# Another order within a tick on VectorE and ScalarE, in the stage that weaves attention into the projections

## The reference

```python
def project(x, norm_mix, w_in, q_norm, k_norm):
    p = rmsnorm(x, norm_mix) @ w_in
    q, k, v, z, xbc, dt_raw = jnp.split(p, [...], axis=-1)
    q = rmsnorm(q.reshape(b, t, N_HEADS_A, HEAD_DIM), q_norm)
    k = rmsnorm(k.reshape(b, t, N_HEADS_A, HEAD_DIM), k_norm)

def dilated_branch_prompt(q, k, v, rel_bias, window, dil):
    logits = jnp.einsum('gnqhd,gnkhd->gnhqk', qb, kb) * ATTN_SCALE
    logits = jnp.where(valid[None, :, None], logits + bias[None, None], -jnp.inf)
    m = jnp.max(logits, axis=-1, keepdims=True)
    pr = jnp.exp(logits - m)
    den = jnp.sum(pr, axis=-1)
    o = jnp.einsum('gnhqk,gnkhd->gnqhd', pr, vb) / jnp.swapaxes(den, 2, 3)[..., None]

def causal_conv(xbc, prior, conv_w, conv_b):
    out = sum(xpad[:, i:i + t] * conv_w[i] for i in range(CONV_WIDTH)) + conv_b
    return jax.nn.silu(out), xpad[:, t:]
```

## Time and profile before

| | us |
|---|---|
| median of 3 runs | 1942.02 |
| lowest and highest | 1933.88, 1943.04 |
| profiled execution | 1942.02 |
| its span | 1940.1 |
| TensorE busy | 1851.5 (95%) |
| VectorE busy | 1405.9 (72%) |
| ScalarE busy | 887.6 (46%) |
| POOL busy | 1099.8 (57%) |

### The profile page before, as it was taken

How to read it: one execution, slowest core, us unless ns; L and a number is a source line. 1 busy time by engine, 2 the same in 40 slices (tenths; PEclk the granted TensorE clock), 3 DMA queues, 4 the chain that set the end, 5 groups by cost and what they waited for, 6 DMA issues and landing times.

```text
span 1940.1 us, 33409 instructions
## 1 busy us (share of the span) xinstructions
PE 1851.5 (95%) x12776; PEld 1700.9 (88%) x12776; DVE 1405.9 (72%) x1897; ACT 887.6 (46%) x1610; POOL 1099.8 (57%) x846
## 2 busy tenths in 40 slices
PE   8999999998888999989997999999999999999999
PEld 7999999887777888855556789989999999999999
DVE  5788830787677766569987655798767779877876
ACT  5433412576566777456663002343333344444442
POOL 4588740777676777424444223335555557777774
PEclk9999999999999999979998999999999999999999
DMA  4444433543443443389995535114343357444442
GB/s 172 148 169 179 172 136 94 126 130 95 109 110 95 134 125 111 113 287 327 328 319 177 185 145 189 73 61 183 123 162 144 137 212 285 149 152 156 143 134 92
DMA packets 139097, 309.31 MB, mean 159 GB/s; under 512 B 31659, under 2 KB 65323, under 8 KB 135228
## 3 DMA queue, kind: packets, MB, share of 16 engines
q1 hardware_dynamic: 114924, 270.60, 41.5%
q10 hardware_dynamic: 24016, 36.58, 5.5%
HBM read 222.42 MB, written 93.28 MB: 163 GB/s over the span
## 4 chain that ended last, share of the span: by engine, by line
PE 58%; DVE 11%; POOL 5%; issue 5%; ACT 3%; DMA 0%; ACTq 0%; DVEq 0%; POOLq 0%
PE ff_ps L2594 31%; PE dense_ps L973 7%; PE wo_psa L2429 5%; POOL att_p L920 3%; PE att_t_ps L1002 2%; PE wo_psb L2561 2%; PE wo_psa L2561 1%; PE att_s_ps L991 1%; PE att_s_ps L992 1%; DVE sa_vlo L1961 1%; POOL w_lo L235 1%; PE ssd_in L1638 1%; DVE silu_half L1118 1%; PE sa_s L1551 1%; DVE ssd_m L1879 1%
## 5 line engine op out<-in xcount | busy, mean ns | idle before, releaser
L2594 PE MATMUL ff_ps<-ff_set,ff_wring 128*128 128x264 f32 x5376 | 661.5, 286 | 8.4 <-DVE ff_set L3206 3.5
L2594 PEld LDWEIGHTS ff_ps<-ff_set,ff_wring 128*128 128x128 f32 x5376 | 658.9, 189 | 10.5 <-DVE ff_set L3206 3.9
L920 POOL TENSOR_SCALAR att_p<-att_p,att_rden 128x128 f32<-128x128 f32 (+7 forms) x128 | 242.3, 1901 | 118.2 <-DVE att_rden L1060 118.1
L2263 POOL TENSOR_TENSOR ff_wring<-const,ff_wring 128x256 fp32r<-128x256 f32 (+1 forms) x192 | 212.6, 1111 | 146.5 <-ACT ff_wring L2759 145.9
L2759 ACT ACTIVATE ff_wring<-const 128x256 fp32r<-128x256 f32 (+1 forms) x192 | 93.5, 489 | 222.0 <-PE ff_ps L2594 108.4
L3228 DVE TENSOR_TENSOR h<-h,ff_ps 128x528 f32<-128x528 f32 x192 | 133.2, 700 | 49.9 <-PE ff_ps L2594 47.1
L1180 ACT ACTIVATE att_pThi<-att_t_ps 128x512 fp32r<-128x512 f32 x192 | 93.5, 487 | 133.6 <-PE att_t_ps L1002 125.3
L1078 DVE CUSTOM_DVE_ANT_0 att_p<-att_s_ps,att_bias 128x128 f32<-128x128 f32 (+7 forms) x128 | 95.3, 754 | 57.8 <-PE att_s_ps L992 51.9
L1065 DVE TENSOR_TENSOR att_pTlo<-att_t_ps,att_pThi 128x512 fp32r<-128x512 f32 x192 | 104.5, 552 | 41.2 <-ACT att_pThi L1180 41.0
L973 PE MATMUL dense_ps<-u_hi,w_hi 128*128 128x352 f32 x480 | 115.0, 341 | 10.3 <-DVE conv_pre L1092 3.1
L2263 POOL TENSOR_TENSOR ff_wring<-wo_raw,ff_wring 128x256 fp32r<-128x256 f32 (+1 forms) x72 | 83.5, 1159 | 61.8 <-ACT ff_wring L2759 61.8
(11 more groups left out here) (366 smaller groups left out, 4316.2 us busy)
## 6 DMA issues: line engine op xcount, KB each, us to landing
tmp_r_sets<-h SPq DMA_DIRECT2D x16, 1848.0 KB, 5.9
ff_setraw<-tmp_r_sets SPq DMA_DIRECT2D x56, 528.0 KB, 5.5
sa_k<-in_cache_k SPq DMA_DIRECT2D x32, 640.0 KB, 8.9
sa_v<-in_cache_v SPq DMA_DIRECT2D x40, 512.0 KB, 4.7
w_raw<-in_w_feat SPq DMA_DIRECT2D x36, 512.0 KB, 6.4
out_qk<-proj_out SPq DMA_DIRECT2D x16, 528.0 KB, 8.0
tmp_bias_rows<-tmp_table ACTq DMA_DIRECT2D x8, 1024.0 KB
att_bias<-tmp_bias_rows SPq DMA_DIRECT2D x16, 512.0 KB, 3.4
```

Source lines behind the costliest of these rows:

```text
L920: pool.tensor_scalar(slot(h, qt), slot(h, qt), rden[:, qt, :], None, ALU.mult).then_inc(normed, 1)
L2263: pool.tensor_tensor(w_set(n)[:, 1], operand(q, m), w_set(n)[:, 0].bitcast(F32), ALU.subtract).then_inc(fw_split, 1)
L2594: mm = pe.matmul(ff_ps[:, (b + g) * 512:(b + g) * 512 + HG], ws[:, wi, k, :], xs[:, xi, k, g * HG:(g + 1) * HG], start=(opens and k == 0 a ...
```

## The change

On VectorE, `keep_low` now comes ahead of `bias_min` in a tick, and `invert` comes ahead of `evict`, `add_out` and `split_v`. On ScalarE, `split_out` comes ahead of `keep_high`. No instruction is added or removed, and the loops of TensorE, POOL and SyncE are as they were.

```diff
@@ VectorE @@
             for n in range(FIRST - 1, END + 1):
                 if n == FIRST + 1:
                     split_v(0)
+                if n in piece:
+                    keep_low(n, *piece[n])
                 for h, qt in score.get(n, ()):
                     bias_min(h, qt)
-                if n in piece:
-                    keep_low(n, *piece[n])
+                if n - 1 in score:
+                    invert(score[n - 1])
                 for d in evict_at.get(n, ()):
                     evict(d)
                 if n in ends:
@@
                 if n >= 0 and h < NH and n % TICKS == 9:
                     split_v(h)
-                if n - 1 in score:
-                    invert(score[n - 1])
                 for d, t in tap_at.get(n, ()):
                     convolve(d, t)
@@ ScalarE @@
+                if n in ends:
+                    split_out(*ends[n])
                 if n in piece:
                     keep_high(n, *piece[n])
-                if n in ends:
-                    split_out(*ends[n])
                 for h, qt in score.get(n - 1, ()):
                     exponent(h, qt)
```

## The result

The changed kernel takes 1962.38 us (median of 6 runs, 1957.66 to 1966.71) against 1940.88 us (6 runs, 1933.88 to 1943.04): ratio 1.0119, 95% interval 1.0103 to 1.0137. By the medians it is slower by 21.5 us, by the ratio by 23 us (20 to 27); 1944.7 us was forecast. The profiled execution took 1962.54 us with a span of 1960.6, so it stands for the median as that of before did.

The account below looks back on a forecast made before the run. TensorE, busy 454.4 of 490 us in the stretch from 340 to 830 us, was taken as the bound. Terms -2.0 + 3.0 - 1.1 + 2.2 - 0.6 + 1.2 = +2.7 on 1942.02 gave 1944.7 us, range 1931 to 1956.

Parts of the forecast that it names:

- R2: Slower: reductions pushed back in VectorE's classes 7 and 9 set each head's pace; 18.6 us, 1960.6 us; chance 0.17.
- part 2, on add_out: On VectorE, the output sum behind the reciprocal: +0.69 us counted at waits for tile 4's reduction, 0 in later heads.
- (b): On VectorE, tile 4's reduction behind `keep_low` of its own tick: +0.6 us for each of five TensorE waits, +3.0.
- Its reading that the rows don't agree on the normalising: POOL's normalising at 589.48 ran beside the tap of 589.31, which still took 1.32 us, so no port exclusion there.
- Part 1 (a): TensorE's transpositions wait less for `keep_low` of two ticks earlier: three of 8 stalls keep their gain, -2.0 us.
- Part 1 (c): `keep_low` fills VectorE's holes before scores, so evictions come earlier at two of three waits for silu_half: -1.1 us.
- Part 2, evictions: Evictions behind `invert` on VectorE: +1.6 us at tick 42, 0.3 each at ticks 109 and 121, sum +2.2.
- Part 3: `split_out` ahead of `keep_high` on ScalarE: split waits' gain 0, eviction at tick 98 later by 1.2 us.
- The argument against R2: VectorE waits 50 times for scores in the stretch, more than three times a head, so is late only in places.
- R2's own test: It decides if TensorE meets the reduction of tile 4 late in more than 8 heads, as 8 x 1.24 = 9.9.
- TensorE's busy time and the granted clock stay.: Expected sign in the profile: no change in TensorE's busy time or granted clock; no us were put on it.
- The prediction's own sign of being wrong: TensorE's waits in the stretch changing by more than 10 us, or its waits for att_min falling.

Follow-up runs that it names:

- the last three edits: Kernel before with class 6's taps ahead of add_out and invert, with no taps in class 8, and with both: 0.9994, 0.9995 and 1.0003.

## Why the prediction was wrong

The forecast was +2.7 us with +24 as the outermost bound; measured is 21 to 23. The case that came true is rival R2 (1960.6 us), which had 0.17. Its mechanism is right in the main, and that its number is so near is in part luck: it priced 18.6 us of waiting, and 14.7 us of waiting came, with 6.7 us of a slower TensorE that no case had.

**The step that failed first: part 2, on add_out: "In the later heads VectorE has room: 0."** It counted 0.69 us inside five waits of (b) and nothing elsewhere. The run with this move alone is 0.69% slower; it lost 13.7 us, 5.6 of them as idle time of TensorE, with 12 hidden waits behind `keep_low` of class 7 in place of 6. The reciprocal waits for an exponent, and everything behind it waits too; the sum filled that hole for nothing, and behind it delays what follows. I looked at whether VectorE has idle time in these heads, which it has, and not at where: it lies ahead of the reciprocal and ahead of the scores of tile 4, and the moved sum falls between them, ahead of tile 7's reduction, whose result ScalarE waits for, and `keep_low`, for which TensorE's next transposition waits. In the head shown the length was off too: 1.21 and 1.26 us instead of 0.68, as the sum now starts beside POOL's w_lo subtraction. In the run with this move alone that subtraction runs from 718.34 for 1.29 us; the sum starts at 718.92 and ends 0.55 after it. In the full change it is 721.81 for 1.30, and 0.54. The Trainium skill (SBUF — State Buffer, "SBUF: two separate sides") says that such a pair exclude each other at their shared port, and here the trace agrees but for 0.14 us, as the 0.54 and 0.55 us left after the subtraction are less than the sum's 0.68. The prediction applied this to the taps, and not to the sum, which it had moved onto that subtraction. Its reading that the rows don't agree on the normalising was wrong: there the normalising paid (the last section has the rows).

**Part 1 (b), 5 x 0.6 = +3.0.** It priced `keep_low` ahead of tile 4's reduction at its own 0.55 us because its input stood ready at 593.95. That was read from a head with a tap there; in a light head the high part comes at ScalarE's pace, and ScalarE's pace hangs on the reduction of tile 7, which the same edit also delays. The price is a wait for the other engine and not a length. With the first head left out, the waits of TensorE for the reduction of tile 4 are not 5 but 13 (one in each of 13 heads), 18.3 of the 22.2 us. `keep_low` alone lost 10.8 us in the stretch, 6.6 of them idle time, and `keep_low` in classes 7 and 9 alone 9.9 and 3.9.

**Part 1 (a), -2.0.** With `keep_low` alone moved the issue waits fell to 0.2 us, as the mechanism says. In the full change they fell to 0.8 (below 1.5 was forecast), but three waits of 3.0 us together stand elsewhere under `keep_low`'s name: 3.8 us in all, in place of 4.5. With the waits for the reduction up by 13.5 nothing was kept. The 0.25 us of start-up that the sum adds to each stall stands in no row; what the rows show is 0.10 us from the end of `keep_low` to the transposition, and that is part of the wait already.

**Part 1 (c), -1.1.** Not there: waits for silu_half rose from 3.0 to 4.3 us; with `keep_low` alone they fell to 2.6.

**Part 2, evictions, +2.2.** The stall at tick 42 was forecast at 1.6 us and is 1.77. The move of `invert` past the evictions alone costs 2 to 9 us, with 3.2 us more idle time; so the forecast may hold or be too low, and which of the other nine evictions costs, the runs don't tell.

**Part 3, +1.2 at tick 98 and nothing else.** Right for the move alone: 1.0005, and the wait of 1.79 became 3.0 there. In the full change it is 3.2. The split's waits (below 2 us was forecast) are 2.0 with the move alone and 4.8 in the full change.

**The argument against R2** was that VectorE still waits 50 times for scores, so it is late only in some places. This took a wait of VectorE as slack. But in a cycle in which each engine waits for the next, every member can show waits, and none of them need be slack: in the kernel after these waits are down to 4.4 us, and the time is up. R2's own test, tile 4 met late in more than 8 heads, was the right one: it was 6 heads before, the first left out, and came out at 13. One light head of the kernel before would have answered it: the slack ahead of tile 4's reduction is 1.12 us (709.07), and the sum (0.68) and `keep_low` (0.55) that now stand ahead of it use 1.23, without any wait for ScalarE.

**"TensorE's busy time and the granted clock stay."** This put a term at nothing without a reason. The busy time rose by 6.7 us for the same work, about a third of the loss. The prediction's own sign of being wrong, TensorE's waits changed by more than 10 us, came as well (14.7). The 10 us of the kernel after in which the granted clock fell most, columns as above:

```profile
580.00:590.00 10.00, 8.19 (x35) 7.33 (x35) 4.72 (x13) 4.93 (x8) 1.96 (x2) 0.66 0.80 227
```

The granted clock is 0.66 over these 10 us, so for part of them it was at the lower of its two levels (1.2 and 2.4 GHz): three dense matmuls take 1.08 us at 585.52 and 0.64 at 588.68. Ahead of it TensorE had stood for 2.41 us, until 581.72. That the clock is lower after the change is not an accident of one profile: its mean over the span is 0.984 in 31 executions of the kernel before (0.985 in 26 on another chip) and 0.981 in 31 of the kernel after. The difference is 0.0026, which over 1942 us is 5 us, an estimate of what this part costs on average. Why it is lower stays open. It does not simply follow the waiting: the three kernels with taps moved waited less than the kernel before, and their clock is 0.983, 0.982 and 0.982 in ten executions each.

## What to carry to other kernels

On an in-order engine, ask of each moved instruction what it waits for and what it used to do during that wait: an instruction with its inputs ready, put behind one that waits, can cost up to its whole length in every repetition in which the next engine is close behind, even on an engine that idles a quarter of the time. Price a move in the plainest repetition of the loop and multiply by its count before looking at the special places; look at more than one, as a single one can be off (0.68 and 1.21 us for the same sum here). Follow it once around all engines, since a delay that returns through another engine's queue can be larger than the instruction. When the waits at the bounding engine are short and have many releasers, expect gains to be taken over by the next releaser. And split a difference into idle time and busy time of the bounding engine before explaining it: here a third of the loss went with its clock, and so did what the last three edits had won.

## What the runs showed of the hardware

A VectorE operation on two SBUF inputs (the sum of the output, a tap, the low part of v, the gate) and a GpSimd operation beside it: the one that starts second mostly pays, and the first keeps its time. These counts are of the woven stretch (340 to 835 us) in the traces of all 14 kernels.

- GpSimd's subtraction first, the sum second: 1.21 us at 722.44 is 0.67 until the subtraction ends at 723.11, and 0.54 after. All 14 sums that had only this subtraction beside them, and started behind it, end 0.54 or 0.55 us after it; they take 1.03 to 1.76 us in place of 0.67 to 0.69. Of 17 taps that started during the subtraction, seven took 1.89 to 2.17 us in place of 1.33; the others kept their time, six of them in the last tenth of a microsecond of the subtraction, four beside subtractions that were themselves stretched to 2.9 us.
- VectorE first: 60 taps beside a normalising and 20 beside the subtraction take 1.31 to 1.33 us, as alone. GpSimd pays: the subtraction of 128x512 takes 1.59 to 2.44 us (123 cases) and 1.26 to 1.31 alone (179), the normalising of 128x384 takes 1.64 to 2.27 (74 cases) and 1.24 or 1.25 alone (100).

So the normalising of the earlier trace rows and its tap are no exception. The tap had started 0.17 us earlier and kept its 1.32 us, and the two normalisings behind it took 3.81 us. The same two without a tap, in the run with `invert` past the evictions:

```profile
464.43 2.79 POOL L920 TENSOR_SCALAR att_p<-att_p,att_rden 128x384 f32<-128x384 f32 x2 [1.29 <-DVE att_rden L1060]
```

One case does not fit a block until the first has ended: of 153 sums that started during a normalising and had nothing else of GpSimd beside them, 92 took 0.70 us or less, their time alone, and the longest took 1.41. What decides between them was not tested.
